# Third modulation summed in the second mixer, first dense layer in two phases by seven products, first tap of a convolution on ScalarE

## What is computed

```python
def swiglu(h, wg, wu, wd):
    ...
cs = jax.nn.silu(c)
for i in range(DEPTH_2):
    mod = cs @ ada_w[i] + ada_b[i]
    sh1, sc1, g1, sh2, sc2, g2 = [m[:, None, :] for m in jnp.split(mod, N_MOD, axis=-1)]
    h = rms_norm(x, norm_mix_g[i]) * (1 + sc1) + sh1
    ...
        mix = hybrid_mixer_2(h, ...)      # layer 0
        mix = conformer_conv(h, ...)      # layer 1
    x = x + g1 * mix
    h = rms_norm(x, norm_ffn_g[i]) * (1 + sc2) + sh2
    x = x + g2 * swiglu(h, ffn_w_gate[i], ffn_w_up[i], ffn_w_down[i])
return rms_norm(x, final_norm_g)
```

## Time and profile before

| | us |
|---|---|
| median of 3 runs | 1463.28 (1461.82 to 1464.57) |
| the profiled execution | 1465.13 |
| its span | 1463.4 |
| first block | 0 to 477 |
| second mixer | 477 to 903.6 |
| first dense layer, first product to end of the last down product | 907.64 to 1128.32 |
| convolution begins (L2869) | 1133.52 |
| second dense layer | 1248.74 to 1455.72 |

### The profile page before, as it was taken

One profiled execution on the slowest core, in us unless ns is written; L12 is line 12 of the kernel. 1 busy time (PEld: TensorE's weight loads), 2 busy tenths in 40 slices (PEclk: granted clock), 3 DMA queues, 4 the chain that ended last, 5 costly groups with the idle time before them and its releaser, 6 DMA issues. The chain is left out here.

```text
span 1463.4 us, 18944 instructions
## 1 busy us (share of the span) xinstructions
PE 1376.3 (94%) x7517; PEld 1015.5 (69%) x7517; DVE 870.7 (60%) x1464; ACT 275.6 (19%) x602; POOL 265.6 (18%) x342
## 2 busy tenths in 40 slices
PE   5999999896776999999999999999999999999997
PEld 1877655653442788768888888777766878888843
DVE  2458775432232668753454685788783874777864
ACT  2222221000000311643345101000002113211101
POOL 5078010000000300553355402100020100000000
PEclk9999999998888999999999999999999999999999
DMA  9976887899999697866774455898854552555431
GB/s 350 310 263 226 285 329 298 348 417 415 416 418 385 191 305 261 306 194 162 159 180 133 160 162 176 327 333 322 297 210 150 155 156 73 163 168 172 170 129 47
DMA packets 176057, 355.58 MB, mean 243 GB/s; under 512 B 7289, under 2 KB 137041, under 8 KB 158561
## 3 DMA queue, kind: packets, MB, share of 16 engines
q1 hardware_dynamic: 166720, 313.64, 60.4%
q0 software_dynamic: 9248, 40.71, 9.5%
HBM read 352.58 MB, written 1.74 MB: 242 GB/s over the span
## 5 line engine op out<-in xcount | busy, mean ns | idle before, releaser
L1846 PE MATMUL PS<-HT,ring 128*128 128x256 f32 x1152 | 258.3, 382 | 0.1
L1846 PEld LDWEIGHTS PS<-HT,ring 128*128 128x128 f32 x1152 | 215.5, 190 | 36.0 <-issue 7.9
L1542 DVE TENSOR_TENSOR X<-X,PS 128x1024 f32<-128x1024 f32 x14 | 17.1, 1222 | 113.2 <-PE PS L1318 113.2
L1265 PE MATMUL PS<-ring_extra,slot_rows 128*32 128x256 f32 x576 | 56.3, 450 | 27.6 <-DMA ring_extra<-in_expert_w_gate 7.1
L2876 PE MATMUL PS<-HT,ring 128*128 128x256 f32 x352 | 76.8, 379 | 0.0
L2905 PE MATMUL PS<-ada_stage,half_sums 128*128 128x256 f32 x320 | 75.6, 379 | 0.0
L2905 PE MATMUL PS<-ring,half_sums 128*128 128x256 f32 x320 | 75.6, 379 | 0.0
L2876 PEld LDWEIGHTS PS<-HT,ring 128*128 128x128 f32 x352 | 66.7, 190 | 9.0
L2882 PE MATMUL PS<-ring,hid 128*128 128x512 f32 x160 | 71.8, 592 | 0.0
L2905 PE MATMUL PS<-ring,HT 128*128 128x256 f32 x304 | 68.8, 379 | 0.0
L2905 PEld LDWEIGHTS PS<-ring,half_sums 128*128 128x128 f32 x320 | 59.4, 190 | 11.2 <-issue 4.3
(11 more groups left out here) (736 smaller groups left out, 2465.4 us busy)
## 6 DMA issues: line engine op xcount, KB each, us to landing
ring<-in_hy_w_in SPq DMA_DIRECT2D x40, 1024.0 KB, 8.4
ring_extra<-in_w_ada SPq DMA_DIRECT2D x24, 1024.0 KB, 7.9
ada_stage<-in_ada_w POOLq DMA_DIRECT2D x24, 1024.0 KB, 7.3
ring<-in_ffn_w_gate SPq DMA_DIRECT2D x22, 1024.0 KB, 5.9
ring<-in_ffn_w_up SPq DMA_DIRECT2D x22, 1024.0 KB, 5.8
ring<-in_ffn_w_down SPq DMA_DIRECT2D x22, 1024.0 KB, 5.8
ring_extra<-in_expert_w_down SPq DMA_DIRECT2D x18, 1024.0 KB, 22.9
ring_extra<-in_expert_w_up SPq DMA_DIRECT2D x18, 1024.0 KB, 20.1
```

The costliest lines, as they stand in the source:

```text
L1265: mm = pe.matmul(PS[e * SLOTS:(e + 1) * SLOTS, 2, j * CW:(j + 1) * CW], hs[:, k, e * SLOTS:(e + 1) * SLOTS], w[e][:, k, :], start=(k == 0) ...
L1542: dve.tensor_tensor(part, part, PS[:, 6:8, :], ALU.add).then_inc(added, 1)
L1846: mm = pe.matmul(dst, w[:, k, half * P:(half + 1) * P], HT[:, k, :], start=(k == 0), stop=(k == KT - 1))
```

## The change

- **Third modulation.** The 24 loads, now on SP's queue among the weights of the mixer, and the 24 additions (`add_third`, table `THIRD_ADDS`) move into steps 14 to 35 of the second mixer. Each load is a pair of vectors' pieces, `THIRD_PIECES`: first the two gates, then shift and scale of the mixer norm, then those of the dense norm. The second and third share one home in `third_acc`, so PE's `sum_third` and `turn_third` come twice, at steps 29 and 36, with a copy on ACT between them and `finish_third` on DVE behind. Loads from the sixth on alternate between two buffers (`stage` and `b_c`). PE waits for the first result before `value(m)` from m = 3 on, and for the second before `out_half(0, 1)`.
- **Second modulation.** Its 16 additions go to steps 1 to 13 and have two buffers.
- **First dense layer.** It runs the second layer's code: two phases, seven products everywhere except for the down product of chunk 10. The sums of weights of its chunk 0 are made in the mixer, between `combine_a(1)` and `combine_b(1)`.
- **Convolution of the mixer.** The first of four taps goes from DVE to ACT (`tap`).
- **Around them.** Four more small loads (20 for 16) at the start of the mixer; the biases of the gates arrive by their own loads in the tail; the first gate's rows stand between the two turns of x; `tap_blocks` is built after the first dense layer.

```diff
+        SECOND_ADDS = [(1, 3), (2, 3), (3, 0), (3, 3), (4, 0), (4, 3), (5, 3), (6, 3), (7, 0)] + [(s, 3) for s in range(7, 14)]
+        THIRD_ADDS = ((14, 1), (15, 2), (16, 3), (18, 0), (19, 1), (20, 2), (21, 0), (21, 3), (22, 1), (23, 1), (24, 0), (24, 3),
+                      (25, 2), (26, 1), (27, 0), (27, 3), (30, 0), (30, 3), (31, 2), (32, 1), (33, 0), (33, 3), (34, 2), (35, 1))
...
+                def fetch_third(n):
+                    if n == 0:
+                        sp.wait_ge(summed, ADDS - 1)
+                    elif n == 6:
+                        sp.wait_ge(used, base + V0 + 3)
+                    else:
+                        sp.wait_ge(third_summed, third_before(n) + 1)
+                    sp.dma_start(third_stage[third_buffer(n)], wv3[:, n % KT, THIRD_PIECES[n // KT], :])\
+                        .then_inc(third_in[third_buffer(n)], 16)
...
+                    if m >= 3:
+                        pe.wait_ge(third_made, 1)
...
+                def sum_third(c):
+
+                    pe.wait_ge(third_summed, THIRD_READY[c])
+                    pe.wait_ge(moved_att, THIRD_MOVED[c])
+                    for g in range(4):
+                        v = third_acc[:, 1 + g // 2, :].rearrange("p (m h k) -> p h k m", h=2, k=KT // 2)[:, g % 2]
+                        mm = pe.matmul(PS[32 * g:32 * g + 32, 7, :], ones[:, 0:32], v, start=True, stop=True,
+                                       tile_position=(0, 32 * g))
+                    mm.then_inc(third_rowsum, 1)
+
+                def turn_third(c):
+                    pe.wait_ge(third_rowcopy, c + 1)
+                    for k in range(KT // 2):
+                        mm = pe.transpose(PS[:, 7, k * P:(k + 1) * P], third_rows[:, k * P:(k + 1) * P], ident[:])
+                    mm.then_inc(third_cols, 1)
...
+                def tap(s):
...
+                    for m in range(2):
+                        tile = 2 * XORDER[s] + m
+                        act.activation(conv_tiles(s)[:, m, :], RX[:, s % 3, m, 0:S], ACT.Identity, scale=convT[:, tile:tile + 1],
+                                       bias=convT[:, CONV * XT + tile:CONV * XT + tile + 1]).then_inc(first_tap, 1)
...
                 combine_a(1)
+                first_gate, first_up = (segs["ffn0"].base + j for j in range(2))
...
+                step(dve.tensor_tensor(t1, up[:, 0:4, :], gate[:, 0:4, :], ALU.subtract))
+                step(dve.tensor_tensor(t2, up[:, 4:8, :], t1, ALU.subtract))
+                step(dve.tensor_tensor(up[:, 0:4, :], up[:, 4:8, :], up[:, 0:4, :], ALU.subtract))
+                step(dve.tensor_tensor(t4, gate[:, 4:8, :], t2, ALU.subtract))
                 combine_b(1)
...
             turn(0)
-            ffn(0, 0, turn_vectors, modulation_rows)
-            modulation_columns()
-            gate_rows(1, 0, 0)
-            pe.wait_ge(gated, 4)
-            turn(1)
+            for e in range(FFN_CHUNKS):
+                split_gate_up(0, e, 0)
+                if e == 0:
+                    turn_vectors()
+            for gi in range(len(DOWN_GROUPS)):
+                split_down(0, gi)
+            whole_down(0)
+            turn_row(1, 0)
+            gate_rows(GATE_MIX, 0)
+            turn_row(1, 1)
...
             pool.wait_ge(small, SMALLS)
+            pool.wait_ge(left, 2 * 4)
             for at, m in enumerate(PE_TILES):
```

More of the change, by code:

```diff
@@ L2059, in _ @@
                             value((k - 3) // 2)
+                    if (s, q) in third_rows_at:
+                        sum_third(third_rows_at[s, q])
+                    if (s, q) in third_turn_at:
+                        turn_third(third_turn_at[s, q])
                 def out_half(pc, part):
@@ L2186, in _ @@
                         act.activation(cv[:], cv[:], ACT.Silu).then_inc(cv_ok, 1)
+                    if q == (1 if s == 1 else 0) and 1 <= s <= NX:
+                        tap(s - 1)
                     if q == 2 and 2 <= s < 2 + NX:
@@ L2358, in convolve @@
                     dve.wait_ge(evac, s + 1)
[L2359 to L2361 removed]
+                    for j in range(1, CONV):
                         for m in range(2):
@@ L2929, in seven @@
                 hs7 = lambda j: [hsum[:, j, k, :] for k in range(4)]
-                ws7 = lambda j: [wsum[:, e % 2, j, k, :] for k in range(4)]
-                arrive(pe, n_g)
-                arrive(pe, n_u)
-                pe.wait_ge(combined, weights_summed(f, e))
-                if e > 1:
-                    pe.wait_ge(combined, row_sum(f, e - 1, 2))
-                product(P2, rows(1, 0), half(gate, 1))
-                product(P1, rows(0, 0), half(gate, 0)).then_inc(used, 1)
-                if e > 1:
-                    pe.wait_ge(combined, row_sum(f, e - 1, 5))
@@ L3007, in split_gate_up @@
-            def split_gate_up(e, norm):
-                n_g, n_u = chunk(1, "g", e), chunk(1, "u", e)
-                gate, up = w_slot(n_g), w_slot(n_u)
-                half = lambda ap, h: [ap[:, 4 * h + k, :] for k in range(4)]
-                rows = lambda h, i: [HT[:, 4 * h + k, i * P:(i + 1) * P] for k in range(4)]
-                hs7 = lambda j: [hsum[:, j, k, :] for k in range(4)]
-                ws7 = lambda j: [wsum[:, (e + 1) % 2, j, k, :] for k in range(4)]
+                ws7 = lambda j: [wsum[(e + 1) % 2][:, j, k, :] for k in range(4)]
@@ L3248, in _ @@
             root(0, 0)
             turn(0, mod[:, 3, :], mod[:, 2, :])
-            act.wait_ge(small, SMALLS)
-            act.activation(cv[:], cv[:], ACT.Silu).then_inc(silu_c, 1)
-            ffn(0)
+            act.activation(idle[:, 0:1], ident[:, 0:1], ACT.Silu)
+            gate_and_move(0)
             act.activation(idle[:, 0:1], ident[:, 0:1], ACT.Sqrt)
-            squares_of_pieces(1, pieces(), x_done, 0, 8)
-            act.wait_ge(moved, M_COLUMNS)
+            squares_of_pieces(1, LAST_PIECES, x_done, 0, 8)
@@ L3564, in _ @@
+            for gi in range(1, len(DOWN_GROUPS)):
+                split_sum_down(0, gi)
+                if gi == 1:
+                    split_halve_rows(0, 2)
+            split_last(0, gate_b)
+            last_pieces(0, gate_b)
             scale_row(0, 8)
-            first_mean(1, 1, 0, 8)
             invert_row(1, 1, 8)
             scale_row(1, 8)
-            dve.wait_ge(made, COLUMNS)
-            columns = PS[:, 2:4, :].rearrange("p a (k n) -> p (a k) n", n=P)
-            for n in range(4):
-                c = columns[:, :, 32 * n]
-                if n % 2:
-                    ins = dve.scalar_tensor_tensor(out=mod[:, n, :], in0=c, scalar=1.0, in1=gains[:, n // 2, :],
-                                                   op0=ALU.add, op1=ALU.mult)
-                else:
-                    ins = dve.tensor_copy(mod[:, n, :], c)
```

695 lines of the change are left out of this document (257 added, 438 removed).

## The result

| | before | changed |
|---|---|---|
| median, us | 1463.52 (1460.27 to 1464.57, 8 runs) | 1471.96 (1467.97 to 1477.85, 8 runs) |
| ratio, 95% interval | | 1.0064 (1.0044 to 1.0083) |
| the profiled execution | 1465.13, span 1463.4 | 1474.42, span 1472.6 |

The forecast was 1460.1 with a range of 1454.5 to 1467.5. The time lies outside the range and on the other side of before.

A forecast was written before the change was run, and what follows sets the result against it. The prediction took PE, busy 94% of the span, to bound the kernel. Its terms summed to -3.2 us, taking the profiled 1465.13 to 1461.9 and the median to 1460.1, with a range of 1454.5 to 1467.5.

The forecast's parts named there:

- Part 1: First dense layer: running the second layer's code, it takes that layer's length plus the small vectors' turn; -13.2 us.
- Part 2: From last down product to convolution: PE idles for DVE before the turn of x, 6.7 us against 5.2; +1.5.
- Part 3: Behind the new 2.8 us idle time before the convolution the clock falls; +1.7 us, bounds 0 and 3.4.
- Part 4: Second mixer: PE's added `sum_third` and `turn_third`, each coming twice, cost their full time; +4.8 us.
- Part 5: Mixer: new PE waits, +0.8 us at the first `sum_third`, +1.3 for four small loads (bounds 0 and 3.3).
- The two waits of 0.63: Second mixer: PE's two waits for DVE shrink, as three additions replace four in four steps; -0.6 of 1.3 us.
- Part 6: Attention: the moved additions mostly fit DVE's slack of 3 us; +0.3 us, bounds 0 and 0.8.
- the third rival: Attention: transfers become the bound, loads taking over 12 us to land; +9, so +5.8, 1469.1 us; chance 0.14.
- The addition's price beside GpSimd: Attention: one DVE addition takes 2.35 us, or 3.09 beside POOL, 0.74 more, still within the slack of 3.
- The last stage: `tap_blocks` now lies beside DVE's taps of the long convolution, whose end has some slack; +0.2 us, bounds 0 and 1.5.
- Small costs at their bounds: Rival 2: clock 3.4, small loads 3.3 and attention's part 2.3 us, so +2.3, 1465.6 us; chance 0.20.
- transfers bind: Rival 3, in attention: DMA engines at 1.07 make loads land late; +5.8, 1469.1 us; chance 0.14.

The follow-up runs named there:

- e1: The changed kernel, with the third modulation's four small loads issued after the first gate's bias and given their own signal; 1464.17 us, ratio 1.0011.
- e4: e3 with each of the third modulation's 24 loads bringing only a quarter of its columns, additions whole; 1456.27 us, ratio 0.9968.
- e9: e3 with both loads and additions of the third modulation cut to a quarter; 1456.02 us, ratio 0.9957.
- e2: The changed kernel, with the second modulation's first two 1 MB loads issued one step later; 1463.66 us, ratio 1.0016.
- e3: The changed kernel with the changes of both e1 and e2; 1464.02 us, ratio 1.0007.
- e11: The changed kernel measured again, nothing altered; 1470.42 us, ratio 1.0055.
- e5: e3 with the third modulation's additions covering only a quarter of the columns, loads whole; 1456.88 us, ratio 0.9971.
- e8: e3 with additions 6 to 15 spread, the first sum over rows two quarters later, and the first gate's products before the first turn of x; 1457.20 us, ratio 0.9974.
- e10: e8 without the spread: additions at the changed kernel's places, 0.75 step apart; 1458.37 us, ratio 0.9977.

## Why the prediction was wrong, step by step

- **Part 1, first dense layer, right.** 207.5 us, and 207.5 to 207.9 in all the profiles: the second layer's row told the first layer's length. The largest term of the sum was exact because it was read from a stage that already ran this code.
- **Part 2, the gap, right.** 6.6 us from the last down product's end to the convolution against a forecast of 6.7; the idle time 2.56 for 2.8.
- **Part 3, the clock behind it, right in kind.** It did not fall there in the changed kernel's two profiles; in e1, e4 and e9 it did and cost 1.6. Of ten profiles with that gap three had the fall, so the term's mean is 0.5 and not 1.7, and the bound of 3.4 wasn't reached.
- **Part 4, PE's new rows, right.** 2.4 each. The second one is the +2.7 of the stretch to the output projection but for 0.3.
- **Part 5, the small loads, the first failing step.** I priced "four at 0.54" with bounds 0 and 3.3, from the queue that they are issued on. It was 6.1 of wait and 4.9 of clock. I didn't ask what else the change puts beside them: the second modulation's loads, which the change moves ahead on SP's queue. Their price stood in no row that I read, because before they weren't there; but GpSimd's stop, 3.06 us for no visible reason, stood in the trace, and a cause that doubles it was in the diff. Without that neighbour the four loads cost next to nothing: 0.2 in e2, below the 1.3 and inside the bounds. And I gave the small loads no fall of the clock, though I had just priced one behind 2.8 us of idle time and had 3.3 as the upper bound here; e1 had the fall behind 1.23 us.
- **The two waits of 0.63,** under-counted: both are gone, and the stretch is 1.4 shorter in e3, where I took 0.6.
- **Part 6, attention, the second failing step.** Forecast 0.8 for the first sum's wait and 0.3 for the additions; measured, beyond the sum and turn of rows, 11.4 in one profile of the changed kernel (7.9 of waits, the rest mostly the lower clock, 0.50 behind the longest), 5.1 to 6.2 in e11 and e3. It is the third rival's mechanism: the awaited load took 20.5 us, over the 12 that I named as the point of decision, and the DMA share was 0.96 where 1.07 was reckoned. But it isn't bound by loads alone, as that rival had it. I had set the slack of 3 us against the addition and, apart from it, against the load. e4 and e5 fit one slack that pays both, in the same slot. The chance of 0.14 rested on 168 + 137 GB/s against 425, and bytes were the wrong measure: the engines were full at 272 GB/s. The Trainium skill (DMA: Bandwidth & Descriptors, Bandwidth) gives about 358 GB/s as the limit of one core. No run here shows that limit: the engines were 0.96 busy at 272 GB/s and 1.01 at 425.
- **The addition's price beside GpSimd:** 2.35 to 3.09 with medians of 2.54 to 2.58 in the changed kernel, within what the earlier trace rows said.
- **The last stage:** 330.2 to 331.6 against 329.9, so up to 1.7, just over the bound of 1.5. PE waits up to 2.1 us before the last block of the convolution's products for a cause that no row names. I didn't test that it is `tap_blocks`.
- **The sum.** Put what the first profile shows in place of the terms: start 11.0 for 1.3, attention's waits 11.4 for 1.1, no fall of the clock for 1.7, -1.4 for -0.6. That makes -3.2 + 9.7 + 10.3 - 1.7 - 0.8 = +14.3. The two spans without the first block differ by 9.2 + 5.4 = 14.6. That profile is a dear one: with e11's start (5.8 + 5.2) and attention (5.1) the same sum is +8.0, near the 8.4 between the two medians. So the start is the larger part of the slowdown and attention the smaller.

The range was too short because the start's 11.0 lay far above its bound of 3.3, and because its upper end took the rivals one at a time. "Small costs at their bounds" and "transfers bind" both come from more megabytes beside what is already there, and came together. (Its lower end counts 0.6 of the two waits twice: 1456.6 - 0.8 - 0.7 is 1455.1, not 1454.5. It changes nothing here.)

## What to carry over

When loads move to another queue or an earlier step, list every other transfer in flight at the new time, small ones above all. A stop in the issuing engine that is there already is a sign of it. A slack on an in-order engine is spent once: add the new work and the longest new wait of a slot, and then compare. Where a stage is made dense by moving work out of another, look for idle time of the full engine at the seams: with the four gate products in the gap of 2.6 us, on top of the mended start and the later sum, two versions that do the whole work (e8 and e10) beat both kernels, at 0.9974 and 0.9977.

## What the runs showed of the hardware

- The granted clock fell behind the same idle time of 2.56 us in some executions and not in others: 1.00 in the changed kernel, 0.76 over 6 us in e1. It also fell behind shorter ones: behind 1.23 us in e1 (0.50 to 0.55 over 492 to 498), and behind the 1.95 us before the first dense layer in e9 (0.60 and 0.55 over 907 to 911) but not in e3 (1.00).
- The issue of one 1 MB load on SP took 0.33 us at its shortest and 5.83 in the dense stretch. GpSimd stood for 2.5 to 3.1 us before it issued its thirteenth small load in the ten profiles without, and for 6.1 to 6.3 us in the three with, two 1 MB loads issued early on SP's queue. So here loads of one engine's queue held up the issue of another's. The Trainium skill (DMA: Bandwidth & Descriptors, Issuing engines are not separate DMA queues) says that DMAs of all issuing engines run on the same 16 DMA engines and interleave, and that issuing from several engines saves only the sequencer's issue time. This case's trace agrees on the first, and shows issue time that was not saved: 6.24 us of it in the changed kernel, with the DMA engines 0.96 busy over 470 to 486.
- From the start of its issue to its landing, a load of the third modulation took from 4.8 to 20.5 us in one execution.
